# The residual of an MLP turned by VectorE and sixteen transfers instead of TensorE and ScalarE

## The reference

```
u = _rmsnorm(h, mlp_norm_g[l])
h = h + jnp.square(jax.nn.relu(u @ w_up[l])) @ w_down[l]
h = _rmsnorm(h, final_norm_g)
```

## Time and profile before

| what | value |
|---|---|
| median of 3 runs | 993.13 us (993.12 to 993.52) |
| the profiled execution, its own time | 994.05 us |
| span of the profiled execution | 992.2 us |
| mean granted TensorE clock | 0.997 of full speed (2.4 GHz) |
| busy: TensorE / VectorE / ScalarE / GpSimd | 981.3 / 623.8 / 475.7 / 525.4 us |
| DMA | 117.49 MB in 93196 packets |

### The profile page before, as it was taken

One profiled execution on the slowest core, in us unless ns is written; L12 is line 12 of the kernel. 1 busy time (PEld: TensorE's weight loads), 2 busy tenths in 40 slices (PEclk: granted clock), 3 DMA queues, 4 the chain that ended last, 5 costly groups with the idle time before them and its releaser, 6 DMA issues.

```text
span 992.2 us, 12733 instructions
## 1 busy us (share of the span) xinstructions
PE 981.3 (99%) x4859; PEld 831.1 (84%) x4859; DVE 623.8 (63%) x930; ACT 475.7 (48%) x754; POOL 525.4 (53%) x625
## 2 busy tenths in 40 slices
PE   9999999999999999999999999999999999999996
PEld 7888888888888888888889988888888888888885
DVE  5782257665373761463668999874872781595696
ACT  4554445554672222443334866564644443453464
POOL 3655555555555884754656788665056037008212
PEclk9999999999999999999999999999999999999998
DMA  7323221212353225233223123377558347536346
GB/s 236 102 77 126 85 86 45 83 43 68 116 173 113 86 85 194 89 104 103 68 85 92 58 65 127 108 253 185 155 170 197 107 147 180 152 86 182 54 85 169
DMA packets 93196, 117.49 MB, mean 118 GB/s; under 512 B 4002, under 2 KB 70080, under 8 KB 93136
## 3 DMA queue, kind: packets, MB, share of 16 engines
q1 hardware_dynamic: 86384, 102.20, 31.4%
q0 software_dynamic: 6448, 14.16, 8.3%
q10 hardware_dynamic: 304, 0.33, 0.1%
HBM read 110.91 MB, written 2.10 MB: 114 GB/s over the span
## 4 chain that ended last, share of the span: by engine, by line
PE 99%; ACT 0%; DVE 0%; issue 0%; DVEq 0%; ACTq 0%
PE ps L582 70%; PE ps L977 15%; PE ps L601 4%; PE ps L727 1%; PE ps L651 1%; PE ps L748 1%; PE ps L712 1%; PE ps L711 1%; PE ps L855 1%; PE ps L1023 1%; PE ps L789 1%; PE ps L634 1%; PE ps L627 0%; PE ps L818 0%; PE ps L951 0%; PE ps L889 0%
## 5 line engine op out<-in xcount | busy, mean ns | idle before, releaser
L2534 POOL TENSOR_TENSOR wlo<-raw,whi 128x256 fp32r<-128x256 f32 x496 | 400.7, 860 | 220.5 <-ACT whi L1031 220.3
L582 PE MATMUL ps<-Hh,whi 128*128 128x512 f32 x512 | 201.6, 394 | 0.0
L582 PE MATMUL ps<-Hl,whi 128*128 128x512 f32 x512 | 199.5, 390 | 0.0
L1031 ACT ACTIVATE whi<-raw 128x1024 fp32r<-128x1024 f32 (+1 forms) x126 | 132.4, 1051 | 91.9 <-PE ps L582 51.4
L582 PE MATMUL ps<-Ah,whi 128*128 128x512 f32 (+1 forms) x496 | 165.2, 359 | 0.0
L582 PE MATMUL ps<-Al,whi 128*128 128x512 f32 (+1 forms) x496 | 163.7, 356 | 0.0
L582 PE MATMUL ps<-Hh,wlo 128*128 128x512 f32 x512 | 129.5, 389 | 0.0
L582 PEld LDWEIGHTS ps<-Hh,wlo 128*128 128x128 f32 x512 | 96.1, 188 | 20.1
L582 PEld LDWEIGHTS ps<-Hh,whi 128*128 128x128 f32 x512 | 96.2, 188 | 19.6 <-DVE Hl L1638 0.2
L582 PEld LDWEIGHTS ps<-Hl,whi 128*128 128x128 f32 x512 | 96.2, 188 | 19.2
L582 PE MATMUL ps<-Ah,wlo 128*128 128x512 f32 (+1 forms) x496 | 104.8, 356 | 0.0
(11 more groups left out here) (372 smaller groups left out, 1673.9 us busy)
## 6 DMA issues: line engine op xcount, KB each, us to landing
raw<-in_w_in SPq DMA_DIRECT2D x29, 1024.0 KB, 5.2
raw<-in_w_up SPq DMA_DIRECT2D x16, 1024.0 KB, 5.5
Fm<-in_w_down SPq DMA_DIRECT2D x8, 1024.0 KB, 5.1
w_w<-in_w_down POOLq DMA_DIRECT2D x16, 512.0 KB, 5.9
raw<-in_w_in SPq DMA_DIRECT2D x14, 512.0 KB, 3.6
raw<-in_w_att_out SPq DMA_DIRECT2D x4, 1024.0 KB, 5.2
raw<-in_w_sg_out SPq DMA_DIRECT2D x4, 1024.0 KB, 5.3
raw<-in_w_o SPq DMA_DIRECT2D x4, 1024.0 KB, 5.1
```

What stands on the lines that cost most here:

```text
L582: mm = e.matmul(ps[:, bk, 0:c1 - c0], of(j)[:, k % kk, 128 * g:128 * g + 128], x[:, k, c0:c1], start=(start and n == 0), stop=(stop and n ...
L1031: return e.activation(out, src, ACT.Copy, scale=scale)
L2534: ins = e.tensor_tensor(w_lo(j)[:, *cut], raw_tile(j)[:, *cut], f(w_hi(j))[:, *cut], ALU.subtract)
```

## The change

x1 is no longer turned by TensorE. VectorE's `transpose`, which turns blocks of 32 by 32 in place of the whole 128 by 128, writes each group of `F3` to `F4f`, in two instructions (128 partitions x 256 elements each), sixteen in all. They stand in VectorE's program of part 0 behind `act(3)` and ahead of `x_sums(P_7)`. The blocks are then on the wrong partitions; sixteen transfers on SyncE's queue, each from 32 partitions to 32 partitions (source: 4 KB in one piece on each; destination: 32 pieces of 128 bytes, 512 bytes apart), move them to `Y`. They wait for the last of VectorE's instructions (`residual_blocks`, 7), stand behind `final_g` and ahead of part 1's `load_block`s, and move 2 MB.

Since `F4f` is now read by the transfers, VectorE waits for all of them (`residual_in`) before `out(P11)` in part 0, its first write to `F4f`. `down_free(P_4)`, which waited for ScalarE's last copies from banks 6 and 7, names `mlp_mean` instead, and ScalarE's casts of down tiles 0 and 1, whose place in memory overlies x1, wait for `residual_blocks` instead of TensorE's transposes.

```diff
+        Y_pieces = F1f.rearrange("p (x c f) -> p x c f", c=4, f=32)
+        turned = F4f.rearrange("p (i x f) -> p i x f", i=4, f=32)
...
@@ sync_program, part 0, behind final_g
+                    w.wait_ge("residual_blocks", 7)
+                    for c in range(4):
+                        for i in range(4):
+                            e.dma_start(Y_pieces[32 * i:32 * i + 32, :, c], turned[32 * c:32 * c + 32, i]).then_inc(
+                                *b.done("residual_in", (c, i), 16))
@@ tensor_program
-            def residual(n):
-                bk = 7 - n % 2
...
-                for i in range(4):
-                    mm = e.transpose(ps[:, bk, 128 * i:128 * i + 128], F3[:, n, 128 * i:128 * i + 128], ident[:])
-                mm.then_inc(*b.done("residual_turned", n))
...
                 if n == P_4:
-                    return "residual_set", 7 - r
+                    return "mlp_mean", 0
...
-                    if part == 0 and 3 <= n < 7:
-                        residual(2 * n - 6)
-                        residual(2 * n - 5)
@@ scalar_program
                 elif m in (0, 1):
-                    w.wait_ge("residual_turned", 7)
+                    w.wait_ge("residual_blocks", 7)
...
-            def residual(n):
-                w.wait_ge("x1_late", 3)
-                w.wait_ge("residual_turned", n)
-                src = ps[:, 7 - n % 2, :].rearrange("p (r t c) -> p r t c", r=2, t=2)
-                copy(Y[:, :, n // 4, :, 128 * (n % 4):128 * (n % 4) + 128], src).then_inc(*b.done("residual_set", n))
...
@@ vector_program
+            def residual(n):
+                to = F4f.rearrange("p (i r c t m f) -> p r c t i m f", i=4, r=2, c=2, t=2, m=4)
+                of = F3[:, n].rearrange("p (r t i f) -> p r t i f", r=2, t=2, i=4)
+                w.wait_ge("products", (J_UP - 1, 3))
+                for r in range(2):
+                    signal = b.done("residual_blocks", n) if r else step()
+                    e.transpose(to[:, r, n // 4, :, :, n % 4], of[:, r]).then_inc(*signal)
...
                     if n != P12 and part == 0:
+                        w.wait_ge("residual_in", (3, 3))
                         e.tensor_copy(y, bank).then_inc(*signal)
                     else:
-                        w.wait_ge(*(("down_out", (part - 1, n, r)) if part else ("residual_set", 7)))
+                        w.wait_ge(*(("down_out", (part - 1, n, r)) if part else ("residual_in", (3, 3))))
                         e.tensor_tensor(y, bank, y, ALU.add).then_inc(*signal)
...
                     if n == 3:
+                        if part == 0:
+                            for m in range(8):
+                                residual(m)
                         x_sums(part, P_7)
```

More of the change, by code:

```diff
@@ L1547, in scalar_program @@
                     cast(up_tile(0, n) + 2)
-                if n < 7:
-                    residual(2 * n - 6)
-                    residual(2 * n - 5)
                 for i in {3: (0,), 4: (1, 2), 5: (3,), 6: (4,)}.get(n, ()):
```

## The result

The changed kernel takes 995.38 us, median of 14 runs (993.46 to 997.05); the kernel before, beside it, 993.33 us (992.91 to 993.99). The ratio is 1.002, with a 95% interval of 1.0012 to 1.0027: slower by 2.0 us, with the interval from 1.2 to 2.7 us. The forecast was 992.0, in a range of 989.3 to 1000.5. The changed kernel also scatters more: 3.6 us between its fastest and slowest run, against 1.1.

The account below looks back on a forecast made before the run. TensorE, busy 99% of the span, was taken as the bound: 3.6 us gained less 2.5 us waiting for the transfers gives 1.1 us faster, 992.0 us from the median of 993.13, range 989.3 to 1000.5.

Parts of the forecast that it names:

- dear pieces: Rival for the sixteen transfers: 128-byte pieces cost 27.3 ns, TensorE stands 15.5 us, 1005.0 us; slower, dear pieces above all, 0.26.
- Given back: Part 1's loads land after 708 with 20 us of room; last accumulating transfer of part 0 counted nothing, up to 1 us.
- What TensorE gains: Four pieces of eight transposes leave TensorE's MLP chain, 3.48 us, plus 0.12 at up tiles: 3.6 us.
- VectorE's transposes: Sixteen on VectorE ahead of `x_sums(P_7)`, 0.33 us each, 5.4 us in all, hidden in idle time; upper bound 10.7.
- The price of a piece: DMA engine time per 128-byte piece of the sixteen: 12.2 to 16.9 ns, taken at 14.6, giving 15.0 us.
- All is hidden: Rival: pieces under 13.8 ns, sixteen land before 707.3, TensorE keeps 2 us or more, at best 989.5 us; chance 0.36.
- The landing: Last of the sixteen lands at 708.2 us (705.7 to 710.6): 681.9 + 2.0 + 15.0 + 9.3 for three accumulating transfers.
- The issues: Sixteen issues on SyncE's queue from about 681.9, 0.68 us each, 11 us, less than the data takes.
- TensorE at P12: TensorE waits ahead of `down(P12)` or in `down(P_6)`, landing 708.2 less 705.7: 2.5 us (0 to 4.9).
- The earlier limit of 705.7: Latest start of VectorE's `out(P11)` so that `w_low(9)` ends when TensorE wants it: 722.6 less 16.9 us of work.
- The clock: Way to fail: TensorE, once it has waited, is granted a lower clock; no size was counted.

Follow-up runs that it names:

- experiment 1: Changed kernel with all part 1 loads on SyncE's queue held until part 0's last accumulating transfer has landed: 989.63 us, ratio 0.9964 to the kernel before.
- experiment 4: Changed kernel without its sixteen transfers, x1 not added; what waited for them waits for VectorE's transposes: 989.07 us, ratio 0.9958 to the kernel before.
- experiment 2: Changed kernel with each of the sixteen transfers' destinations one 4 KB piece a partition, residual in wrong order: 991.64 us, ratio 0.9981 to the kernel before.
- experiment 7: Changed kernel with only part 1's w_down quarters, not its weight blocks, held until the last accumulating transfer landed: 990.88 us, ratio 0.9975 to the kernel before.
- experiment 3: Kernel before with part 1's loads held until `out(P11)` of part 0 is done, no small transfers: 997.83 us, ratio 1.004 to the kernel before.

## Why the prediction was wrong

Its sign was wrong: 1.1 us faster was forecast, 2.0 slower measured. The time lies within the range, but by luck: the range reached so far for dear pieces, and the pieces were not dear. The step that failed is the one under "Given back", on the last accumulating transfer: "I count nothing for it, and up to 1 us where the stall exists already." It cost 3.86 us of waiting at `down(P_6)` and 1.49 us of half clock behind it, since it was issued late (behind `out(P11)`) and landed late (beside the loads). Without it the changed kernel would lie at about 995.4 - 5.35 = 990.0, and experiment 1, which removes only that, gives 989.63.

- *What TensorE gains*: 3.6 us forecast; 3.63 us between the chains of before and of experiment 4.
- *VectorE's transposes*: a step of 0.33 us and 5.4 us in all forecast; 5.33 us, and hidden, as forecast.
- *The price of a piece*: 12.2 to 16.9 ns, taken at 14.6. The DMA view of the changed kernel from 682 to 690 us has it:

```profile
q1 hardware_dynamic: 5823, 0.74, 60.7%
q0 software_dynamic: 291, 0.56, 46.5%
```

  60.7% of 8 us on 16 engines over 5823 packets is 13.3 ns. The rival of dear pieces (27.3 ns) falls: 128, 256, 512 and 1024 bytes stand at 13.3, 16.9, 27.3 and 47.2 ns, with no jump in between. The Trainium skill ("DMA: Bandwidth & Descriptors", Specifications) says that under 512 bytes the engine reads, modifies and writes; these rows show no step there. The price is also below the 13.8 ns under which the rival "All is hidden" was to hold, with 2 us or more kept. As far as P12 goes it held: TensorE lost 1.15 us there and would have kept 2.4. It failed by the same step as the forecast.
- *The landing*: 26.3 us after the first issue forecast (708.2 - 681.9), 25.5 measured (706.3 - 680.8). The two accumulating transfers beside the sixteen that the view of 684 to 700 us has took 6.8 us instead of 5.9. That they add to the sixteen was right: with 13.3 ns the sum gives 2.0 + 13.6 + 9.3 = 24.9 us.
- *The issues*: 11 us forecast, 22.64 measured. Most took about 0.70 us each, but six took 1.6 to 3.5 us. In experiment 2, with 32 pieces a transfer instead of 1024, the sixteen still took 14.28 us. Why the queue stalls was not tried. The sum did not hang on it, but what stands behind did: I had noted that the loads would land after 708, and had looked only for their own users, at 728.20.
- *TensorE at P12*: 2.5 us forecast for P12 and `w_low(9)` together (0 to 4.9), 1.15 measured, at P12. The earlier limit of 705.7, from `w_low(9)`, never came to act here, since VectorE was by then held by `w_low(8)`; in experiment 7, where it was not, TensorE waited 0.23 us there too.
- *The clock*: named as a way to fail, not counted; 1.49 us.

Why was 1 us the bound? I had the number that should have warned: ScalarE had already waited 2.88 us for that transfer in the kernel before, so nothing lay between its landing and `w_low(8)`. Behind that TensorE had about 1 us of slack at `down(P_6)` (`out(P12)` began at 720.03 and takes 0.6 us a bank, `down(P_6)` began at 721.66), and 0.26 us at `w_low(9)`. The chain from `out(P11)` over `w_low(6)`, issue, landing and cast to `w_low(8)` was a second path as tight as VectorE's own, and 4.2 MB of loads at the 322 GB/s of the view from 709 to 720 us (3.54 MB in 11 us) are 13 us of full engines put right beside its 5.9 us. The prediction worked out neither that path nor those bytes.

## What to carry to other kernels

When work is inserted into a transfer queue, list what stands behind it and ask not only when those transfers are needed but beside what they will now run: pushed together, they slow a transfer on another queue that has no slack. A step for which an engine already waits in the profile before is on a path of its own, and needs its own sum. Here one more wait, ahead of loads that had 20 us of room, took the changed kernel from 995.38 to 989.63 us, against 993.73 for the kernel before. And two delays on one path, each nearly covered by slack, can cost several times their sum: here 6.2 us against 2.1.

## What the runs showed of the hardware

- SBUF to SBUF, from 32 partitions to 32, large pieces were not cheap. In experiment 2 the sixteen moved 512 pieces of 4 KB; the DMA view from 681 to 697 us, in which they and a few kilobytes of loads lie, has

```profile
DMA packets 1320, 3.16 MB, mean 197 GB/s; under 512 B 281, under 2 KB 297, under 8 KB 1320
...
q1 hardware_dynamic: 776, 2.11, 59.4%
```

  so 59.4% of 16 us on 16 engines is 152 us of engine time, close to 0.3 us a piece, or 9.5 us of each engine, where 1024 pieces of 128 bytes at 13.3 ns take 13.6. A 32nd of the pieces saved less than a third of the time. Why a piece of 4 KB costs so much there was not tried.
- After 3.70 us of idle time TensorE ran at a mean clock of 0.54 for the next 3.3 us (1.49 us lost); after 2.85 us in experiment 3 the next eight matmuls took 2.09 us, at a granted clock of 1.00. Each was seen once.
- An accumulating transfer of 512 KB from GpSimd's queue takes 5.5 to 5.9 us alone, and 9.0 to 9.8 us beside loads that fill the engines.
